# The opening of a two-layer transformer kernel: Strassen sums of the normed input made from turned quarters on POOL and DVE instead of turned by PE

## What is computed

```python
h = rms_norm(x, norm_mix[l])
proj = h @ w_in[l]
aq, ak, av, rq, rk, rv, rg, ga, gr = jnp.split(proj, offsets, axis=-1)
```

## Time and profile before

| | us |
|---|---|
| median of 3 runs | 2598.3 (2596.51 to 2602.94) |
| the profiled execution, its own time | 2598.22 |
| its span in the profile | 2596.4 |
| PE busy | 2561.8 (99% of the span) |
| DVE busy | 1572.9 (61%) |
| POOL busy | 1239.0 (48%) |
| ACT busy | 1047.1 (40%) |

### The profile page before, as it was taken

How to read it: one execution, slowest core, us unless ns; L and a number is a source line. 1 busy time by engine, 2 the same in 40 slices (tenths; PEclk the granted TensorE clock), 3 DMA queues, 4 the chain that set the end, 5 groups by cost and what they waited for, 6 DMA issues and landing times.

```text
span 2596.4 us, 35463 instructions
## 1 busy us (share of the span) xinstructions
PE 2561.8 (99%) x13134; PEld 2139.7 (82%) x13134; DVE 1572.9 (61%) x2598; ACT 1047.1 (40%) x2073; POOL 1239.0 (48%) x988
## 2 busy tenths in 40 slices
PE   8999999999999999999999999999999999999998
PEld 6888888777888988888888878998888888888886
DVE  7355554685535554454698751168667666587787
ACT  4332343584223332332444541169733322254443
POOL 2478784354535565555221774448444544200204
PEclk9999999999999999999999999999999999999999
DMA  6557674705541222221752344323233333364534
GB/s 216 193 184 282 227 260 155 275 18 196 186 181 63 78 86 90 81 82 66 283 191 94 110 154 177 89 67 84 64 119 106 114 106 108 120 252 132 185 102 166
DMA packets 162711, 372.41 MB, mean 143 GB/s; under 512 B 21538, under 2 KB 42658, under 8 KB 158882
## 3 DMA queue, kind: packets, MB, share of 16 engines
q1 hardware_dynamic: 162540, 370.15, 41.7%
HBM read 268.01 MB, written 101.83 MB: 142 GB/s over the span
## 4 chain that ended last, share of the span: by engine, by line
PE 73%; DVE 3%; POOL 2%; DMA 1%; ACT 1%; issue 1%; POOLq 0%; SPq 0%; DVEq 0%; ACTq 0%
PE PS L841 9%; PE PS L844 9%; PE PS L843 9%; PE PS L906 6%; PE PS L907 6%; PE PS L908 6%; PE PS L650 3%; PE PS L652 3%; PE PS L651 3%; PE PS L672 3%; PE PS L675 3%; PE PS L674 3%; PE PS L1028 2%; PE PS L1017 1%; PE PS L977 1%
## 5 line engine op out<-in xcount | busy, mean ns | idle before, releaser
L2332 POOL TENSOR_TENSOR WL<-WRAW,WH 128x512 fp32r<-128x512 f32 (+1 forms) x149 | 248.4, 1668 | 310.8 <-ACT WH L1087 310.7
L841 PE MATMUL PS<-HH,WL 128*128 128x512 f32 (+1 forms) x976 | 369.0, 378 | 2.1 <-POOL WL L2332 2.1
L843 PE MATMUL PS<-HL,WH 128*128 128x512 f32 (+1 forms) x976 | 367.0, 376 | 0.0
L844 PE MATMUL PS<-HH,WH 128*128 128x512 f32 (+1 forms) x976 | 367.0, 376 | 0.0
L1604 DVE TENSOR_TENSOR WL<-TS,WH 128x512 fp32r<-128x512 f32 x228 | 235.6, 1042 | 193.5 <-ACT WH L1087 193.4
L906 PE MATMUL PS<-WH,DAL 128*128 128x512 f32 x756 | 294.7, 390 | 0.8 <-DVE WL L1878 0.8
L908 PE MATMUL PS<-WH,DAH 128*128 128x512 f32 x756 | 294.4, 389 | 0.0
L907 PE MATMUL PS<-WL,DAH 128*128 128x512 f32 x756 | 294.4, 389 | 0.0
L2516 POOL TENSOR_TENSOR X<-X,DV 128x512 f32<-128x512 f32 x56 | 90.1, 1634 | 354.4 <-DVE DV L1992 270.2
L1087 ACT ACTIVATE WH<-TS 128x512 fp32r<-128x512 f32 x228 | 138.4, 622 | 214.2 <-POOL TS L2348 214.1
L2348 POOL TENSOR_TENSOR TS<-WRAW 128x512 f32<-128x512 f32 x114 | 152.4, 1336 | 136.5 <-issue 132.9
(11 more groups left out here) (421 smaller groups left out, 6085.6 us busy)
## 6 DMA issues: line engine op xcount, KB each, us to landing
WRAW<-in_u_f SPq DMA_DIRECT2D x56, 512.0 KB, 3.6
WRAW<-in_u_in SPq DMA_DIRECT2D x54, 512.0 KB, 4.3
WRAW<-scr_t SPq DMA_DIRECT2D x52, 512.0 KB, 3.7
scr_h<-HS SPq DMA_DIRECT2D x96, 256.0 KB, 2.3
WRAW<-in_u_gu SPq DMA_DIRECT2D x44, 512.0 KB, 3.5
scr_t<-TTa SPq DMA_DIRECT2D x18, 1024.0 KB, 4.1
WRAW<-in_u_out SPq DMA_DIRECT2D x24, 512.0 KB, 3.6
scr_x<-X SPq DMA_DIRECT2D x24, 512.0 KB, 4.9
```

The source lines that it names most:

```text
L841: e.matmul(PS[:, b, 0:wd], wl[:, blk(kk)], op_moving(q, kk, c0, wd, 0), start=(kk == 0), stop=False)
L843: e.matmul(PS[:, b, 0:wd], wh[:, blk(kk)], op_moving(q, kk, c0, wd, 1), start=False, stop=False)
L844: mm = e.matmul(PS[:, b, 0:wd], wh[:, blk(kk)], op_moving(q, kk, c0, wd, 0), start=False, stop=(kk == 3))
L2332: e.tensor_tensor(lo, raw, hi.bitcast(F32), ALU.subtract).then_inc(*c.inc("w_lo_p", i))
```

## The change

1. `sums0` and `turn0` of the three engines go. PE does no L727 transposes.
2. POOL, directly behind its eight roots and ahead of unit 6's low term, adds high and low terms of tiles 0 to 3 back together into `X`, 8 instructions of 512 wide: these are the turned quarters A11 and A12 as whole numbers.
3. DVE's new `sums0(j)`: S3 from `X` and the bank of `back(1, j+4)` that holds turned A21, S2 from the bank with turned A22 minus S3. These two instructions, not the low terms, now give the two banks back. For tiles 4 to 7 the low terms of `back` count up another semaphore instead. `sums0(j)` stands behind DVE's `back(1, 6)` for j = 0 and `back(1, 7)` for j = 1.
4. POOL's `sums0(j)`, in its program at rv tiles 6 to 9: S4 = A12-S2, then S1 = S2+A11.
5. ACT writes the high terms (`high_term`) and DVE the low ones (`low_term`) from `X` by the table `HIGH_AT`; the low term now reads two SBUF operands, where it read PSUM and SBUF.
6. PE waits for these low terms ahead of the first block's products; ACT's first two P1 results wait for S1's low terms, as their buffer lies over `X`.
7. The identity's DMA is issued ahead of the second row tile's DMA, not behind.

```diff
-    TURN_AT = {i: 2 if i > 13 else 1 for i in range(6, 16)}
+    HIGH_AT = {4: [("S3", 0), ("S2", 0)], 5: [("S3", 1), ("S2", 1)], 6: [("S3", 2), ("S2", 2)], 7: [("S3", 3), ("S2", 3)],
+               9: [("S4", 0)], 10: [("S4", 1)], 11: [("S4", 2)], 12: [("S4", 3)],
+               13: [("S1", 0)], 14: [("S1", 1)], 15: [("S1", 2), ("S1", 3)]}
...
@@ dve_program
-                                hh.bitcast(F32), ALU.subtract).then_inc(*bk.free(key))
+                                     hh.bitcast(F32), ALU.subtract)
+                lo.then_inc(*(c.inc("s_ov", (tt, b2)) if k == 1 and tt > 3 else bk.free(key)))
...
         def sums0(j):
+            for half in range(2):
+                w.wait_ge(*c.at("s_op", (j, half)))
             for b2 in range(2):
+                w.wait_ge(*c.at("s_ov", (j + 4, b2)))
+            key = "nb", 1, j + 4, 0
+            for q, b2, left, right in (("S3", 0, whole0("A11", j), None), ("S2", 1, None, whole0("S3", j))):
+                key = "nb", 1, j + 4, b2
+                ps = by_tile(PS[:, bk.at(key), :])
+                e.tensor_tensor(whole0(q, j), ps if left is None else left, ps if right is None else right,
+                                ALU.subtract).then_inc(*bk.free(key))
+                w.wait_ge(*bk.out(key))
...
@@ pool_program
         n_split[0] = 6
+        for tt in range(4):
+            for half in range(2):
+                hh, hl = [t[:, 4 * half:4 * half + 4, blk(tt)].bitcast(F32) for t in (HH, HL)]
+                w.wait_ge(*bk.out(("nb", 1, tt, half)))
+                w.wait_ge(*bk.full(("nb", 1, tt, 1)))
+                e.tensor_tensor(whole0(("A11", "A12")[half], tt), hh, hl, ALU.add).then_inc(*c.inc("s_op", (tt, half)))
...
         for i, key in enumerate(RVG):
             if i < 15:
                 feed(key)
+            if 6 <= i < 10:
+                sums0(i - 6)
             down_sums(key)
...
@@ sync_program
             if t == 0:
                 e.dma_start(GB[:, :], bcast(a["norm_mix"], D)).then_inc(*c.inc("gb0", 1, 16))
-            if t == 1:
                 e.dma_start(ID[:, :], a["c_id"]).then_inc(*c.inc("c_id", 0, 16))
```

More of the change, by code:

```diff
@@ L439, in bcast, with whole0, sum0_done @@
         return bass.AP(row.tensor, row.offset, [[0, P], [1, n]])
-    def rows0(q, j):
-        tt, half = {"S1": (j + 4, 1), "S2": (j, 0), "S3": (j + 4, 0), "S4": (j, 1)}[q]
-        return X[:, tt, hs(half)]
+    def whole0(q, j):
+        tt, half = {"A11": (j, 0), "A12": (j, 1), "S3": (j + 4, 1), "S2": (j + 4, 0), "S4": (j, 1), "S1": (j + 4, 0)}[q]
+        return by_tile(X[:, tt, hs(half)])
+    def sum0_done(q, j):
+        return bk.out(("nb", 1, j + 4, 0 if q == "S3" else 1)) if q in ("S2", "S3") else c.at("s_op", (1, j, q))
     def by_tile(rows):
@@ L523, in build @@
     PROD = [("P1", "A11"), ("P6", "S2"), ("P7", "S3"), ("P5", "S1"), ("P2", "A12"), ("P4", "A22"), ("P3", "S4")]
-    TURN0 = [(q, j) for j in range(4) for q in ("S2", "S3", "S4")]
     TURN = ["A11", "S3", "S1", "S2", "S4", "A12", "A22"]
@@ L692, in normed @@
                 for b2 in range(2):
-                    w.wait_ge(*bk.out(("nb", k, tt, b2)))
+                    w.wait_ge(*(c.at("s_ov", (tt, b2)) if k == 1 and tt > 3 else bk.out(("nb", k, tt, b2))))
         back(1, 0)
@@ L721, in pe_program @@
                 back(1, 1 + x)
[L723 to L730, removed]
         for i, (_, nh, tt) in enumerate(RVG):
@@ L736, in pe_program @@
                 back(1, 3 + i)
[L737 to L740, removed]
         def ret_scores(s):
@@ L836, in strassen @@
                     for j in range(c0 // P, (c0 + wd) // P):
-                        if lay or q[0] == "S":
+                        if lay == 0 and q[0] == "S":
+                            w.wait_ge(*c.at("s_ov", ("lo", q, j)))
+                        elif lay:
                             w.wait_ge(*bk.out(("nb", k, q, j)))
@@ L1138, in act_program, with high_term @@
             first_square(4 + x)
[L1140 to L1145, removed]
+        def high_term(q, j):
+            if q == "S4":
+                w.wait_ge(*c.at("s_op", (1, j, "S1")))
+            if q == "S1":
+                w.wait_ge(*bk.full(("rv", 1, j + 4)))
+            w.wait_ge(*sum0_done(q, j))
+            e.activation(op_cols(q, j, 0), whole0(q, j), ACT.Copy).then_inc(*c.inc("h_hi", (1, q, j)))
         for i, key in enumerate(RVG):
@@ L1150, in act_program @@
                 back(1, 3 + i)
-            for _ in range(TURN_AT.get(i, 0)):
-                turn0(*turned0.pop(0))
             if i < 15:
                 feed(key)
-        for j in range(4):
-            turn0("S1", j)
+            if i == 4:
+                w.wait_ge(*c.at("n_x", (1, NT - 1)))
+            for q in HIGH_AT.get(i, ()):
+                high_term(*q)
         nr, n1 = len(R1), len(A1)
@@ L1228, in act_program @@
                         w.wait_ge(*c.at(f"h11_{par(m)}", (0, m - 2)))
+                    else:
+                        for j in range(4):
+                            w.wait_ge(*c.at("s_ov", ("lo", "S1", j)))
                     w.wait_ge(*bk.full(key))
@@ L1674, in dve_program @@
                 sums0(i - 3)
-            for _ in range(TURN_AT.get(i, 0)):
-                turn0(*turned0.pop(0))
             if i < 15:
                 feed(key)
-        for j in range(4):
-            turn0("S1", j)
+            for q in LOW_AT.get(i, ()):
+                low_term(*q)
         nr, n1 = len(R1), len(A1)
```

33 lines of the change are left out of this document (15 added, 18 removed).

## The result

| | before | after |
|---|---|---|
| median, in one comparison | 2599.2 us (2596.51 to 2602.94, 4 runs) | 2614.98 us (2613.61 to 2617.16, 4 runs) |
| the profiled execution | 2598.22 | 2613.84 |
| its span | 2596.4 | 2612.0 |

The ratio is 1.0067, with a 95% interval of 1.0055 to 1.0079: the change costs 15.8 us. In the three later comparisons, with 17 to 31 runs of it, the kernel before has a median of 2597 us; against that the change costs some 18 us. The profiled execution after is 1.1 us under its median, the difference of the two spans is 15.6 us.

What follows compares the result with a forecast made beforehand. PE, busy 99% of the span at full clock, was taken as the bound. Terms -6.9 + 14.8 + 2.5 + 1.5 + 0.2 = +12.1 us on 2598.3 gave 2610.4 us; range 2597 to 2616.

Steps and rivals of the forecast that it cites:

- everything else, at nothing: Remaining DVE, POOL and ACT work costs nothing; after the opening all engines shift alike; late low terms could cost 8 us.
- the restart: After PE's long stop ahead of rv tile 4, about seven matmuls run slowly: 1.5 us lost, between nothing and 3.
- The worst case: All terms at their costly bounds: -6.9 + 16.7 + 2.5 + 3.0 + 0.5 = +15.8 us.
- The port is the bound: Rival: POOL and DVE alternate on the shared port over the whole opening, low terms come late; 2614 us, chance 0.14.
- What PE no longer does: 16 groups of 4 transposes leave PE, with 9 restarts behind single groups: 6.9 us gained.
- The wait that takes its place: Additions delay unit 6's low term, rv tile 1's store, ACT's put and bank 2; rv tile 4 starts 14.8 us later.
- The second bank: rv tile 5 waits for bank 5, given back by DVE's S3 of j = 1: 2.5 us lost.
- The identity: At the start, its earlier DMA delays the second row tile: +0.2 us, bounds -0.3 and +0.5.
- Only the bank waits: Rival: rv tile 1's store is not delayed; rv tile 4 3.7 us late, tile 5 2.5; 2597.7 us, chance 0.13.
- The change does what it says: Rival: PE never waits for a bank, 6.9 us gained minus 0.2; 2591.5 us, chance 0.08.

Runs made afterwards that it cites:

- run 1: The changed kernel, with POOL making unit 6's low term ahead of its eight additions; 2602.7 us, ratio 1.0022.
- run 5: The changed kernel, with SP storing rv tiles 0 and 1 ahead of its load of unit 9; 2603.47 us, ratio 1.0022.
- run 10: The changed kernel, with PE making the transposes of tile 6 thirteen times over, the result the same; 2614.97 us, ratio 1.0068.
- run 6: The kernel before, with only the identity's DMA moved ahead of the second row tile's; 2598.19 us, ratio 1.0003.
- run 3: The changed kernel, with unit 6's low term ahead of POOL's additions and DVE's sums of j = 0 and 1 early; 2596.32 us, ratio 0.9998.
- run 4: As run 3, with the identity's DMA back behind the second row tile's; 2595.75 us, ratio 0.9994.
- run 8: As run 4, with POOL making the weight sums first and S4 and S1 behind them; 2591.62 us, ratio 0.9980.
- Run 2: The changed kernel, with DVE's sums of j = 0 and 1 ahead of tile 6's low terms, POOL's order unchanged; 2605.79 us, ratio 1.0034.
- runs 7: As run 4, with PE's transposes of the first pair's attention values two products later; 2591.11 us, ratio 0.9977.
- run 9: As run 4, with S4 and S1 behind POOL's weight sums and the attention value transposes two products later; 2590.32 us, ratio 0.9974.

## Why the prediction was right or wrong

The sign and the mechanism of the main term were right: slower, by the store that SP holds behind unit 9's load. The step that failed is *everything else, at nothing*: POOL's chain of weight sums does not move with PE, and 2.0 us were lost in the first block. Beside it the restart was sized at half of what it cost (1.5 for 2.95 us). The forecast of 2610.4 us was 4.6 us under the measured 2614.98; 3.5 us of that are terms (12.1 said, 15.6 between the two spans), the rest is that the profiled execution lies 1.1 us under its median. The first product, said for 127.5 us, came at 128.99.

The bounds have a slip. The worst case, +15.8 us, gives 2598.2 + 15.8 = 2614.0 us, not 2615 or 2615.8. So the measured 2614.98 lies 1 us above the forecast's own terms at their worst, and inside the range only because that was drawn to 2616 by the slip and by the port rival, which did not happen. That the time fell into the range is partly luck. Step by step:

- **What PE no longer does**: 6.9 us said, 7.3 measured. The 0.4 us between them lie in the matmuls behind each group, of which I counted only the first gap. From the group at 59.12 to the next at 65.04 are 5.92 us, and a tile without a group takes 5.44 (54.40 / 10): a group costs 0.48 us where I had 0.45, and the pair 0.93 where I had 0.81.
- **The wait that takes its place**: 14.8 us said, 14.63 measured, rv tile 4 at 57.05 where I had 56.6, with the difference in the late opening. Of its links, POOL's additions took 10.9 (11.1 said; one of them took 2.29 us, the shortest 1.26, and the last norm, which begins beside the first of them, takes 2.30 us instead of 3.41), the store left at 49.16 (48.8 said) and took 4.7 us (4.8 said). Runs 1 and 5 show by two different edits, one in POOL's order and one in SP's, that this is the cause.
- **The second bank**: 2.5 us said, 2.69 measured.
- **The restart** is the term that was sized too small: 1.5 us said for one restart, 1.52 and 1.43 measured for two. I had put the slow pace on the long stop alone and let tile 5's stop of 2.44 us pass without one. The pace itself was read rightly from the earlier trace rows. The Trainium skill, "TensorE: Matmul & The Clock Gate", What's actually happening, says that an idle array falls back to the lower clock; the trace agrees (0.50 from 57 to 60 us), and run 10's rows show that the fall can come after work has begun again.
- **The identity**: 0.2 us said, bounds -0.3 and 0.5; 0.64 measured in the changed kernel, 0.51 in run 6. Both lie at or just above my upper bound; that the DMA is an eighth of a tile's was no guide to what it costs the tile behind it.
- **Everything else, at nothing** is the step that failed: nothing said, 2.0 us measured. I wrote that after the opening all engines are shifted alike, because weight loads and buffers are released by PE's own progress. POOL's chain of weight sums is not, as the table shows. "Sum" is the start of the first of the fourth group of four `TS` sums on POOL, "product" the first product on PE; the last but one column is distance - 64.31 - 1.45, since before DVE's `HS` was ready 1.45 us ahead of the transposes that use it (184.79 and 186.24 us).

| kernel | product | sum | distance | wait worked out | wait measured |
|---|---|---|---|---|---|
| before | 115.41 | 179.72 | 64.31 | none | none |
| the change | 128.99 | 196.53 | 67.54 | 1.8 | 1.84 |
| 1 | 116.64 | 183.76 | 67.12 | 1.4 | 1.43 |
| 3 | 108.68 | 178.13 | 69.45 | 3.7 | 3.69 |
| 4 | 108.02 | 177.65 | 69.63 | 3.9 | 3.84 |
| 5 | 118.57 | 185.57 | 67.00 | 1.2 | 1.31 |
| 8 | 107.93 | 175.15 | 67.22 | 1.5 | 1.53 |
| 10 | 129.12 | 198.80 | 69.68 | 3.9 | 3.61 |

The rows behind the first two lines, from POOL's and PE's timelines, of the kernel before

```profile
179.72 1.29 POOL L2348 TENSOR_TENSOR TS<-WRAW 128x512 f32<-128x512 f32 x1 [4.57 <-issue]
186.24 1.04 PE L861 MATMUL PS<-ID,HS 128*128 128x128 f32 x8
```

and of the change, there with what stands ahead of the sum on POOL and in SP's queue:

```profile
189.95 1.84 POOL L2331 TENSOR_TENSOR WL<-WRAW,WH 128x512 fp32r<-128x512 f32 x1
191.87 0.33 SPq L2734 DMA_DIRECT2D WRAW<-in_u_in  x1
196.53 1.28 POOL L2347 TENSOR_TENSOR TS<-WRAW 128x512 f32<-128x512 f32 x1 [4.74 <-issue]
201.71 1.06 PE L857 MATMUL PS<-ID,HS 128*128 128x128 f32 x8 [1.84 <-DVE HS L1796]
```

The chain has a pace of its own. POOL's low term ends at 191.79 us and frees a slot of `WRAW`, SP issues the load into it at 191.87, the load lands 4.5 us later, and POOL's sums begin at 196.53. From group to group that gives 19.88 us in the change (176.65 to 196.53), 19.89 in run 4 and 19.69 in the kernel before, about 15.1 of it POOL's work and the rest the load. Nothing in these rows waits for PE, so a group that is late stays late.

One number, how far POOL's sums lie behind the first product, gives the wait in seven kernels to 0.3 us. (Run 2 is not in the table, as its PE had stood for POOL before that place; in runs 7 and 9 the transposes stand elsewhere.) Part of the distance is S4 and S1 ahead of the weight sums: putting them behind (number 8 against 4) took 2.4 us off it. That is one execution each, and the distance can differ by as much between executions: the change and run 10 have the same program on POOL, and 67.54 and 69.68 us. The medians, 2591.62 and 2595.75 us over 11 runs each, carry the comparison. My cover for them, POOL idle for 27 of 49 us, was real and did not help, since the chain does not make up what it is late: in run 4 it is 5.1 us behind its old distance at the third group (157.76 - 108.02 against 160.03 - 115.41) and 5.3 at the fourth. I had priced the late low terms of S2 at up to 8 us; PE did not wait for those.

**The rivals.** *The port is the bound*, 2614 us, is nearest in time and is not what happened: the additions took 10.9 us and not 13. What it says is in the trace, though without effect on PE. DVE's low terms in the timeline of the changed kernel, alone and beside POOL:

```profile
68.23 0.69 DVE L1668 TENSOR_TENSOR S3L<-X,S3H 128x512 fp32r<-128x512 f32 x1
...
76.07 1.75 DVE L1668 TENSOR_TENSOR S3L<-X,S3H 128x512 fp32r<-128x512 f32 x1 [5.22 <-ACT S3H L1143]
```

POOL is idle at the first and works from 70.75 us on. The second takes 1.1 us longer than the first. The Trainium skill, "SBUF — State Buffer", SBUF: two separate sides, says that a POOL instruction that reads SBUF and a DVE instruction with two SBUF inputs exclude each other; the trace agrees with 0.69 and 1.75 us.

*Only the bank waits* is run 1: I had 2597.7, it took 2602.7. Its wait was as said (3.61 us for 3.7). The slow restart (1.3 us: tile 4 took 6.88), the identity (0.4 us more than said) and the first block (1.43 us of wait) come to some 3 of the 5.0 us; the rest is not placed. *The change does what it says*, 2591.5 us, wants DVE's sums early and POOL's additions behind unit 6; built as run 9, with the first block mended too, it takes 2590.3.

## What to carry to other kernels

Before new work is put ahead of an instruction on an engine with room, follow that instruction's result into the DMA queue: what stands behind the waiting DMA moves too, though it has nothing to do with it. A gain at the start of a kernel can be lost again where PE meets a chain that did not start earlier by as much, like POOL's weight sums here; compare the distance between the two streams before and after, not the idle time of the engine. And look for the one consumer that comes early: moving it by two products was worth as much as making the chain faster.

## What the runs showed that I had not expected

- **A short stop can cost as much again.** In the changed kernel a stop of 2.44 us was followed by seven matmuls at half pace, 1.43 us. Over the kernels of this study, stops of 0.97 to 2.03 us had no slow matmul behind them. Those of 2.12 (run 2), 2.37 (run 5), 2.44 (the change, run 10), 3.58 (run 2), 3.61 (runs 1 and 10), 3.69 (run 3), 3.84 (run 4), 3.95 (run 10), 4.24 (run 5) and 14.39 us (the change) had 6 to 10. The exceptions are one stop of 2.44 us in run 1, with none, though it looks in every row like the one in the change, and the 2.21 us of run 2, with none. So the length alone does not decide; what does stays open and was not tried further. It seems to differ between executions of one kernel too: the twelve of run 1 take 2597.99 to 2607.87 us, with mean granted clocks from 0.998 for the two shortest to 0.994 and 0.995 for the two longest, and the one profiled is the second shortest (2599.64 us). So a stop without slow matmuls in one trace is no proof that it never has them.
- **The slow stretch has a size of its own.** After 14.39 us as after 2.44 us it is seven matmuls 0.43 us apart, and six to ten in all cases, 1.2 to 2 us of loss. It may begin 1 us after PE has gone on working (runs 2, 5 and 10). The granted clock falls at 46 to 47 us in the changed kernel, some 4 us into the stop that began at 42.66, and at 58 us in run 10, 5 us behind the start of the stop and 1 us behind its end. Keeping PE at work for 11.5 of the 15 us did not shorten it.
- **So a wait made shorter can win more than its length.** From run 4 to run 8 the wait of 3.84 us shrank by 2.3, and another of 1.26 us appeared, which is 1.05 us less waiting. The time fell by 4.1 us. The rest is the restart: ten matmuls of 0.20 us more and transposes of 1.94 instead of 1.07 us, 2.9 us.
